# Two heads at a time in the attention loop, and another order for the preparation and the periods of the delta rule

## The reference

```
h = rms_norm(x) * (1 + sc1) + sh1                       # scales and shifts from silu(c) @ w_mod
qa,ka,va, qb,kb,vb, zb, a,b, ga,gb = split(h @ w_in)
o_a = attention: 8 heads x 64. context: softmax(q k') v over 128 keys
      latent: softmax(q k' + bias, masked) v over 256 keys of a band and 128 context keys
qd,kd,vd = silu(conv5([qb,kb,vb])); l2_norm and rotary on qd,kd      # 4 heads x 128
o_b = gated delta rule, forward and backward, with a 128x128 state per head and direction
      per chunk: T = (I + A)^-1 (A strictly lower), u = T v, w = T k, S = S*decay + k'(u - w S)
x = x + g1 * ((sigmoid(ga)*(o_a @ w_proj_a) + sigmoid(gb)*(rms(o_b)*silu(zb) @ w_proj_b)) @ w_out)
x = x + g2 * moe(norm(x))                               # top 1 of 4 groups, top 2 of 8 experts
```

## Time and profile before

| | |
|---|---|
| median of three executions | 1285.4 us (1282.55 to 1290.32) |
| profiled execution | 1288.67 us, span 1286.8 us |
| PE / DVE / ACT / POOL busy | 1148.9 / 454.7 / 326.2 / 169.5 us |
| attention loop | about 171 to 423 us of the span |
| delta rule | 423 to 613 us |
| gates, projections, second norm | 613 to 970 us |
| experts | 970 to 1245 us |

### The profile page before, as it was taken

The page is one execution under the profiler, slowest core; times in us unless marked ns, Lnnn a source line. Parts: engine busy times, 40 slices in busy tenths (PEclk is TensorE's granted clock), DMA queues, the critical chain, the costliest instruction groups (busy, mean ns, idle before and its releaser), DMA issues.

```text
span 1286.8 us, 15882 instructions
## 1 busy us (share of the span) xinstructions
PE 1148.9 (89%) x6262; PEld 614.9 (48%) x6262; DVE 454.7 (35%) x874; ACT 326.2 (25%) x587; POOL 169.5 (13%) x260
## 2 busy tenths in 40 slices
PE   2699999999999879989999999999649999999990
PEld 1344456666664659879444444444333333333320
DVE  1223026777763665644431200224431111111115
ACT  4012134454452423342321000112102111111111
POOL 1000020011000254570100000000110111111100
PEclk9699999999989999999999999999859999999995
DMA  8801233333301210210231111150616999999936
GB/s 324 359 1 74 90 125 129 131 138 140 132 1 66 58 29 22 89 24 1 94 130 66 66 49 38 44 196 33 245 43 249 382 395 379 369 392 376 379 109 249
DMA packets 44192, 199.99 MB, mean 155 GB/s; under 512 B 18320, under 2 KB 23904, under 8 KB 32080
## 3 DMA queue, kind: packets, MB, share of 16 engines
q1 hardware_dynamic: 28544, 142.56, 28.9%
q10 hardware_dynamic: 4608, 30.18, 6.3%
q0 software_dynamic: 10960, 26.17, 5.7%
HBM read 190.69 MB, written 22.87 MB: 166 GB/s over the span
## 4 chain that ended last, share of the span: by engine, by line
PE 75%; DVE 10%; DMA 9%; issue 3%; ACT 2%; POOL 1%; SPq 0%; DVEq 0%; POOLq 0%; ACTq 0%
PE bank L1657 24%; PE bank L2202 10%; PE bank L1761 8%; PE bank L2223 6%; DMA arena<-h_scratch,arena 4%; PE bank L2059 3%; PE bank L2057 3%; PE bank L1810 2%; PE bank L1747 2%; PE bank L2190 2%; PE bank L1615 2%; PE bank L1916 1%; PE bank L1718 1%; DMA arena<-in_w_blocks 1%; PE bank L1630 1%
## 5 line engine op out<-in xcount | busy, mean ns | idle before, releaser
L1657 PE MATMUL bank<-arena 128*128 128x512 f32 x720 | 316.2, 595 | 3.9 <-DVE arena L1115 3.0
L1657 PEld LDWEIGHTS bank<-arena 128*128 128x128 f32 x720 | 135.4, 190 | 169.3 <-issue 168.2
L2202 PE MATMUL bank<-arena 128*32 128x512 f32 x1536 | 172.8, 601 | 1.3 <-DVE arena L1570 1.3
L1761 PE MATMUL bank<-arena 128*128 128x320 f32 x384 | 122.2, 452 | 0.5 <-ACT arena L819 0.5
L2202 PEld LDWEIGHTS bank<-arena 128*32 128x32 f32 x1536 | 48.3, 110 | 108.2 <-issue 108.2
L2223 PE MATMUL bank<-arena 128*32 128x512 f32 x768 | 87.4, 595 | 0.8 <-ACT arena L1055 0.8
L1761 PEld LDWEIGHTS bank<-arena 128*128 128x128 f32 x384 | 68.7, 194 | 26.4 <-issue 2.1
L1583 DVE TENSOR_TENSOR arena<-arena,bank 128x256 f32<-128x256 f32 x24 | 10.1, 421 | 176.2 <-ACT arena L1049 176.2
L707 POOL DMA_INDIRECT y_scratch<-arena x24 | 24.3, 1014 | 249.1 <-DVE arena L1576 249.1
L1448 DVE TENSOR_TENSOR arena<-arena,bank 128x512 f32<-128x512 f32 x10 | 6.9, 688 | 135.8 <-PE bank L2059 135.8
L978 ACT ACTIVATE arena<-bank 128x512 f32<-128x512 f32 x20 | 11.9, 597 | 151.5 <-PE bank L1657 151.4
(11 more groups left out here) (297 smaller groups left out, 1502.5 us busy)
## 6 DMA issues: line engine op xcount, KB each, us to landing
arena<-in_w_up SPq DMA_DIRECT2D x32, 2048.0 KB, 10.6
arena<-in_w_blocks SPq DMA_DIRECT2D x27, 2048.0 KB, 8.0
arena<-in_w_down ACTq DMA_DIRECT2D x28, 1024.0 KB, 9.2
arena<-y_scratch SPq DMA_DIRECT2D x10, 512.0 KB, 7.6
arena<-in_bias POOLq DMA_DIRECT2D x3, 1536.0 KB, 11.8
arena<-in_w_down SPq DMA_DIRECT2D x4, 1024.0 KB, 7.8
arena<-in_x SPq DMA_DIRECT2D x5, 512.0 KB, 8.9
gram_scratch<-arena SPq DMA_DIRECT2D x10, 256.0 KB, 2.4
```

The lines of the kernel that those rows point to most:

```text
L1657: last = mm(bank, hT[:, k, tok0[i]:tok0[i] + P], w[:, k, :], start=(k == 0), stop=(k == KC - 1))
L1761: last = mm(banks[5 + half][:, 0:HTOK], w[:, k, :], hT[:, k, half * HTOK:(half + 1) * HTOK], start=(k == 0), stop=(k == KC - 1))
L2202: last = mm(banks[2 + e % 2][at, :], rowsT[e % 2][:, k, at], eup[expert % SLOTS_W][:, k, :], start=(k == 0), stop=(k == KC - 1))
```

## The change

In the attention loop heads are treated two by two: `scores(e)` issues the products of both heads beside each other (they lie on the two halves of the partitions), `values(e)` alternates between the two heads (they write the two halves of bank 3), DVE evicts both before it goes on, and ACT takes both exps in a row. The conv pipeline runs at longer lags. `head_sums` goes: ACT squares each tile by itself and sums it in the same instruction (5 instructions for one). Three of the five `scaled` (L1280 before), `tap(11, 4)` and `silu_out(11)` move ahead of the barrier. In the delta rule the solves move by one period (DVE takes p = 0 and 1 ahead of period 0, POOL 2, 3 and 4, each a period earlier), the row exps are parted from the decay exps, the silu of z goes to the end of the loop, and the first gate product goes ahead of the second barrier.

```
                 if name == "gb0":
                     gram_out(0)
                     blocks_in(0)
+                    solved_out(0)
                     gram_out(1)
+                    solved_back(0)
                     blocks_in(1)
-                    solved_out(0)
-                    solved_back(0)
-                    gram_out(2)
                     solved_out(1)
                     solved_back(1)
+                    gram_out(2)
                     blocks_in(2)
                     solved_out(2)
-                    sp.wait_ge(S["spread"], 2)
                     solved_back(2)
                     for d in range(2):
                         sp.wait_ge(S[f"step{d}"], step_at(0, "st"))
                         sp.dma_start(t["new_state"][d], unit[d]["cstate"]).then_inc(S["cstates_out"], 16)
                     gram_out(3)
+                    blocks_in(3)
...
             for p in range(T):
-                if p == 0:
-                    solve(1, 0, SUB - 1)
-                else:
+                if p:
                     masks(p, 3)
                 if p + 1 < T:
                     q_scaled(p + 1)
-                if 2 <= p < T - 1:
-                    solve(p + 1, 0, SUB - 1)
-                if p + 1 < T:
                     masks(p + 1, 1)
                     spread_out(p + 1)
                     masks(p + 1, 2)
+                if p + 2 < T:
+                    solve(p + 2, 0, SUB - 1)
...
                     act.wait_ge(S["rope_done"], c)
-                step(sc.activation(sq_b, qkv[:, :, c * P:(c + 1) * P], ACT.Square), "sq_ready")
-
-            for u in range(NU):
+                for i in range(T):
+                    step(sc.activation(sq_b[:, i, :], qkv[:, i, c * P:(c + 1) * P], ACT.Square, accum_out=qkstat[:, i, c:c + 1]),
+                         "sq_ready" if i == T - 1 else "act_step")
...
+            for e in range(0, NU, 2):
...
+                exp_out(e)
+                exp_out(e + 1)
+                probs_out(e)
...
+                for u in units_of(e):
+                    if u % 4 == 0 and 4 <= u <= 32:
+                        part_out(3 + u // 4)
+                    if conv_chunk(u, 9) is not None:
+                        silu_out(conv_chunk(u, 9))
+                    if conv_chunk(u, 13) is not None and conv_chunk(u, 13) < 2 * H_B:
+                        head_squared(conv_chunk(u, 13))
...
+                probs_out(e + 1)
+            silu_out(11)
             barrier(act, 1)
...
             kq_out(0)
             decay_exp(0)
+            z_out(1)
+            z_out(2)
             kq_out(1)
             kq_out(2)
-            z_out(2)
+            row_exp(1)
+            kq_out(3)
+            kq_out(4)
...
                     values_kept(p - 1)
+                inv_out(p, 2)
                 coupled(p, 2)
+                if p == 0:
+                    decay_exp(2)
...
-                if p == T - 2:
-                    for i in range(T):
-                        step(sc.activation(z_gate[:, i, :], z_gate[:, i, :], ACT.Silu), "zs_ready")
                 if 1 <= p < T - 2:
+                    row_exp(p + 2)
                     decay_exp(p + 2)
+            for i in range(T):
+                step(sc.activation(z_gate[:, i, :], z_gate[:, i, :], ACT.Silu), "zs_ready")
...
-            def head_sums(c):
-                dve.wait_ge(S["sq_ready"], c + 1)
-                step(v.tensor_reduce(qkstat[:, :, c:c + 1], sq_b, AX_X, ALU.add), "sqsum")
...
                 if part == 0:
+                    dve.wait_ge(S["sq_ready"], c + 1)
                     dve.wait_ge(S["b_in"], 16)
...
+            for e in range(0, NU, 2):
+                evicted(e)
+                evicted(e + 1)
+                if e % 4 == 2 and 6 <= e <= 34:
+                    j = 4 + (e - 6) // 4
                     mod_cols(j, j + 1, banks[4], 0)
...
+                    scaled_probs(u)
+                    if conv_chunk(u, 5) is not None:
+                        tap(conv_chunk(u, 5), 1)
+                    if conv_chunk(u, 6) is not None:
+                        tap(conv_chunk(u, 6), 3)
+                if e >= 2:
+                    pv_out(e - 2)
...
+                for u in units_of(e):
+                    for part in range(3):
+                        if conv_chunk(u, 14 + part) is not None and conv_chunk(u, 14 + part) < 2 * H_B:
+                            rotated(conv_chunk(u, 14 + part), part)
...
+            mod_scales(1)
+            for i in TURNS[:3]:
+                scaled(i)
             pv_out(NU - 1)
...
+            solve(0, 1, 9)
             decay_pre(1)
-            scaled(2)
-            scaled(3)
+            solve(0, 9, SUB)
             gram_out(1)
-            solve(0, 1, SUB)
+            dve.wait_ge(S["kqT_ready"], 2 * T)
             intra_out(1)
...
             first_spread()
-            decay_pre(2)
-            gram_out(2)
+            solve(1, 1, SUB)
...
                 corrected(p, 1)
                 if p == 0:
-                    solve(2, 1, 11)
+                    decay_pre(2)
...
                 corrected(p, 2)
                 if p == 0:
-                    solve(2, 11, SUB)
+                    gram_out(2)
...
+            def scores(e):
+                pair = units_of(e)
+                if e >= 2:
+                    pe.wait_ge(S["max_ready"], e)
...
+                    q = [qaT[rows_, a, SEQ + m * P:SEQ + (m + 1) * P] for rows_ in lanes]
+                    for u in pair:
+                        k = kaT[lanes[u % 2], a, SEQ:TOK].rearrange("p (r c) -> p r c", c=GRID_W)[:, :, BAND_START[m]:BAND_START[m] + BAND_W]
+                        mm(banks[u % 2][:, 0:BAND].rearrange("p (r c) -> p r c", c=BAND_W), q[u % 2], k, start=True, stop=True)
+                    for u in pair:
+                        mm(banks[u % 2][:, BAND:KEYS], q[u % 2], kctxT[lanes[u % 2], a, :], start=True, stop=True).then_inc(S["score_mm"], 1)
...
+            def values(e):
+                pair = units_of(e)
+                pe.wait_ge(S["probT_ready"], e + 2)
+                if e >= 2:
...
+                for a in range(n):
+                    for u in pair:
+                        hc = slice((u % 8) * D_HA, (u % 8 + 1) * D_HA)
+                        vals = va0[:, hc] if e < 8 else vband[:, m % 2, a, hc] if a < 2 else vctx[:, hc]
+                        last = mm(banks[3][64 * (u % 2):64 * (u % 2) + 64, 0:P], vals, probT[:, u % 2, a * P:(a + 1) * P], start=(a == 0), stop=(a == n - 1))
+                        if a == n - 1:
+                            last.then_inc(S["pv_mm"], 1)
...
+            for e in range(0, NU, 2):
...
+                filler(e, 0)
+                filler(e, 1)
+                prob_turn(e)
+                if e >= 2:
+                    values(e - 2)
+                filler(e + 1, 0)
+                prob_turn(e + 1)
+                if e + 2 < NU:
+                    scores(e + 2)
+                else:
...
             key_key(1)
-            kq_turn(3)
-            kq_turn(4)
+            z_mm(4, 0)
             pe.wait_ge(S["kqT_ready"], 2 * T)
             key_query(1)
...
-                turn_inv(p, 2)
                 if p >= 1:
                     new_values(p - 1)
+                turn_inv(p, 2)
                 couple(p, 2)
                 if 1 <= p < T - 1:
                     key_query(p + 1)
                 correct(p, 2)
+                if p == 0:
+                    key_key(2)
...
             key_state(T - 1)
+            first_gate(0)
             new_values(T - 1)
+            first_gate(1)
             read_out(T - 1)
```

254 lines of the change are left out of this document (107 added, 147 removed).

## The result

The changed kernel takes 1249.59 us (median of four, 1248.64 to 1249.91), the kernel before, on the same chip, 1284.74 us (1282.55 to 1290.32): ratio 0.9719, 95% interval 0.9687 to 0.9750. That is 35 us where 47 were forecast; the time lies in the range, 12 us behind its middle. The profiled execution has a span of 1248.1 us.

The account below looks back on a forecast made before the run. PE bounds the kernel (busy 1148.9 of 1286.8 us). Attention's context units 2, latent units 16, loop end 10 and delta rule 20 make 48 us off 1288.7, less 3.3: about 1238 us, range 1220 to 1264.

Parts of the forecast that it names:

- rival A: Attention pairs: row groups don't overlap, or weight loads of small products serialize them; 1248 us, chance 0.15.
- 16 us of the latent units: Attention, units 8 to 35: 23.2 us from overlapped pairs plus 4.8 of idle, less 12 of new waits; pair 11.2 us.
- 4.8 us of idle for the turned chunk: Attention loop: with the longer lag the turned conv chunk no longer waits for its silu, saving 4.8 us.
- 12 us of the squares' ping-pong: Attention loop: rotation and ACT's squares wait on each other, costing PE 1 us a pair over 12 pairs.
- B: Attention loop: DVE and ACT become the bound, a pair stays at 12.35 us; 1254 us, chance 0.17.
- D: Attention loop: squares' ping-pong with one serial chain lengthens every pair beyond 14.4 us; slower, about 1295 us, chance 0.04.
- E: Attention loop: DVE's late evictions are covered, a pair takes 10.4 us; 1226 us, chance 0.12.
- 8 us earlier: Delta rule start: with the new order of solves, DVE's first solve and correction come 8 us earlier.
- Rival C: Delta rule: POOL holds the periods, so the stage gives 8 us in place of 20; 1250 us, chance 0.12.
- 4 us of stall of period 0 go: Delta rule, period 0: decays and a Gram matrix replace the old DVE solve that held PE 4.49 us; 4 us saved.
- Silu, 4.5 us: Delta rule, period 3: moving the silu of z out removes PE's 2.85 us wait and half-speed products; 4.5 us saved.
- New values, 3 us: Delta rule: new values moved ahead of the inverse's turn fill PE's waits for DVE's correction; 3 us saved.

Follow-up runs that it names:

- delta_old: The changed kernel with the delta rule in the old order and the first gate behind the barrier, attention still in pairs: 1261.45 us, ratio 0.9795.
- own_squares: The changed kernel with the squares of the heads' norms written to a place of their own, so ACT doesn't wait for the rotation: 1245.06 us, ratio 0.9684.
- masks_late: The changed kernel with POOL's third masks of period 0 and scaled q made only after the first correction: 1245.34 us, ratio 0.9674.
- all four further edits: The changed kernel with POOL's step 0 masks late, solve of step 1 cut in two, last spread first, and squares in their own place: 1236.45 us, ratio 0.9622.

## Why the prediction was right in its direction and 12 us off

**Attention: right in the sum, with some luck inside it.** 28 us forecast for the stretch to the barrier (2 + 16 + 10), 26.7 measured in one profile and 27.9 in the other, 25.5 by `delta_old`. The pairs overlap on halves of the array, row groups too, which no row of before showed: rival A falls.

The 16 us of the latent units were 23.2 + 4.8 - 12. The 23.2 hold. Of the 4.8 us of idle for the turned chunk only the wait of 2.0 us at 376 went; between 206 and 373 us there were 2.8, and 3.1 stand there now, because the silu still comes late: that step failed. The 12 us of the squares' ping-pong came to about 10, by my estimate: 6.5 us of PE's waits and 3.4 for two low stretches, which no term held. The five squares take some 2.2 us (4 x 0.43 + 0.31 + 0.19), not 3.3. So two terms were 2 to 3 us off and cancelled. That the ping-pong is real `own_squares` shows: without the wait for the rotation the time is 4.5 us less, though 5.8 of DVE's 9.4 us stay. Of the signs given, "no half clock between 373 and 400 us" failed: one stretch now lies at 365 us, and in the first profile one lies at the barrier, 395.9 us. A pair of 11.28 us leaves no room for rivals B and D (12.35 and more) nor for E (10.4).

**Delta rule: 12 us measured where 20 was forecast, and its step "8 us earlier", for the first solve and correction, is the first that failed.** Couple(0,1) came 5.0 and 7.6 us earlier than before in the two profiles, where 9 to 11 was forecast. I laid the instructions one behind the other on DVE with durations taken from a place where POOL was idle, and did not hold POOL's masks against them. Two such products exclude each other. That put 3.1 us on the first chain and a low clock behind it; with the masks moved, couple(0,1) falls into the forecast. Rival C, POOL holding the periods by its third masks, is not what happened: PE never waits for them. Two of the three waits come through DVE; only the one for the last spread is POOL's own.

**"4 us of stall of period 0 go": failed.** The solve of step 1 stands ahead of the correction on DVE and PE waits 2.6 and 3.8 us for it in the two profiles, in the very place where it waited 4.49. I had this solve in my own sum (to +41.4, correction at +42.8) and put it against PE's 34 us of work, not against the correction's due time. From couple(0,1) to couple(1,1) `masks_late` takes 22.3 us, 21.4 before: the stall is 1 us shorter (3.50 us for 4.49), and `key_key(2)`, 1.95 us, which the change moves into this period and which I left out there, has come in. Part of the old stall was the same exclusion (the products of 0.88, 1.03 and 0.93 us at 476 to 479), which the prediction put down to the solve alone. Cutting the solve only moves the wait to `key_key(2)`. What bounds this stretch is the chain of two solves on one engine.

**Silu, 4.5 us: failed; worth nothing that can be seen in this kernel.** The last spread on POOL came 2.79 and 0.49 us late and covered it. I had it about 2.5 us late and charged 1, since "POOL waited in that place" before: a lateness already hidden by the silu was charged at its old price and the silu credited in full. With one of two parallel waits gone, the other one is the time.

**New values, 3 us: right in its mechanism, between 2 us (trace) and 3.5 us (median). Gate, 1 us: right as far as can be told (1.9 by the medians, within the spread; 1.1 us of waits on PE).** The statement that the second barrier comes 170 us behind the first forgot that the gate's 7 us stand between them now.

**The clock was missing.** The prediction counted low stretches as removed (5.1 us at the end of the loop) and never as added. In the first profile each new wait of 2.4 to 2.8 us on PE has one behind it, so a wait of 2.8 us with 3.4 us at half speed cost about 4.5. With all four further edits the clock stays high and key_state(4) comes at 161.8 us, where the forecast has 161.6: its time for the delta rule could be had, but not with this order alone.

## What to carry to other kernels

When work moves under other work, look at which engines run in the same microseconds, not only at each engine's own row: GpSimd's big products hold VectorE's small ones for their full length, and the row of a small operation beside a large one may already be in the profile of before, as it was here. A wait that is removed is worth the distance to the next latest event in that place, so price two parallel waits together. Where TensorE's stalls are a few microseconds each, count them with the low clock behind them, and expect single edits to show less than their share: here two gave nothing that could be told, two gave 4.2 and 4.5 us, and the four together 13.

## What the runs showed of the hardware that was not expected

- A VectorE product with two SBUF inputs that starts while GpSimd runs a 128x512 product ends 0.01 to 0.02 us after it, 1.0 to 1.1 us instead of 0.15; a one-input sum of the same size takes 0.15. A `scaled` of 1.22 us took 2.07, and a copy of 32x256, started while a mask ran on POOL, took 0.70 instead of 0.37. A GpSimd mask beside a `scaled` took 2.12 us instead of 1.2.
- Products of two row halves of the array, in different banks, overlap whole without interleaving (0.72 us for four passes against 0.71 interleaved); column halves issued one behind the other lose a quarter of a microsecond (1.15 against 0.88 us for twelve) and still overlap in part, as one head's six passes take 0.87. By the Trainium skill, "TensorEngine Tiling (Array Packing)", Key Properties, tiles run independently of each other; the runs agree in full for the row halves and in part for the column halves.
- Two executions of one kernel differ in where the granted clock falls (3.4 and 6.8 us behind the same wait), and a stage by 2.6 us with it.
